# Delta heads of a hybrid decoder trunk: two places in ScalarE's order, the places of four weight sums, and the engine that makes the first mixer's

## The reference, cut to what matters

```
u = _rmsnorm(h, norm_mix[layer]).astype(jnp.float32) * valid
(a_q, a_f, a_i, a_g, b_qkv, b_beta, b_decay, b_g,
 c_q, c_k, c_v, c_gk, c_g, gate_logits) = jnp.split(u @ w_in[layer], split_points, axis=-1)
...
def _gated_deltanet(qkv_in, beta_in, decay_in, g_in, conv_w, a_log, dt_bias, norm_w, valid):
    qkv = jax.nn.silu(_causal_conv(qkv_in, conv_w))
    q, k, v = jnp.split(qkv, [B_HEADS * B_DK, 2 * B_HEADS * B_DK], axis=-1)
    q = _l2norm(_split_heads(q, B_HEADS)) * (B_DK ** -0.5)
    k = _l2norm(_split_heads(k * valid, B_HEADS))
    ...
    o = _chunk_gated_delta(q, k, v, log_a, beta)
    return _gated_head_norm(o, g_in, norm_w)
...
gates = jax.nn.sigmoid(gate_logits.reshape(b, total, N_BRANCH, d))
proj = jnp.einsum('blne,ned->blnd', ys, w_branch[layer])
merged = jnp.sum(gates * proj, axis=2)
```

## Time and profile before

| what | value |
|---|---|
| median of 3 runs | 1083.44 us (1082.18 to 1084.93) |
| the profiled execution, its own time | 1080.85 us |
| its span | 1079.0 us |
| PE busy | 1029.5 us, 95% |
| DVE busy | 536.2 us, 50% |
| ACT busy | 309.4 us, 29% |
| POOL busy | 68.4 us, 6% |

### The profile page before, as it was taken

The page is one execution under the profiler, slowest core; times in us unless marked ns, Lnnn a source line. Parts: engine busy times, 40 slices in busy tenths (PEclk is TensorE's granted clock), DMA queues, the critical chain, the costliest instruction groups (busy, mean ns, idle before and its releaser), DMA issues. The chain is left out here.

```text
span 1079.0 us, 20473 instructions
## 1 busy us (share of the span) xinstructions
PE 1029.5 (95%) x8841; PEld 695.6 (64%) x8841; DVE 536.2 (50%) x1074; ACT 309.4 (29%) x573; POOL 68.4 (6%) x73
## 2 busy tenths in 40 slices
PE   9999999999999999999999999999998999887886
PEld 8676776786777877867846546544456665545544
DVE  5757565749469468478464455432344321111124
ACT  3545445334244333343333033010110111101013
POOL 3000000000000000000000000000001222211110
PEclk9999999999999999999999999999999999989899
DMA  9222222141331232132112212163937999999976
GB/s 265 68 66 60 59 61 79 41 100 43 80 70 53 60 83 61 40 84 61 51 49 74 64 42 78 39 272 123 388 122 286 415 413 414 415 416 416 416 305 244
DMA packets 111965, 174.73 MB, mean 162 GB/s; under 512 B 9011, under 2 KB 87100, under 8 KB 103554
## 3 DMA queue, kind: packets, MB, share of 16 engines
q1 hardware_dynamic: 99010, 134.93, 36.3%
q10 hardware_dynamic: 7136, 27.33, 6.4%
q0 software_dynamic: 5728, 11.14, 3.9%
HBM read 169.16 MB, written 12.60 MB: 168 GB/s over the span
## 5 line engine op out<-in xcount | busy, mean ns | idle before, releaser
L767 PE MATMUL ps<-arena 128*128 128x256 f32 x672 | 165.0, 388 | 0.0
L767 PEld LDWEIGHTS ps<-arena 128*128 128x128 f32 x672 | 121.2, 190 | 16.4
L800 PE MATMUL ps<-arena 128*128 128x512 f32 x288 | 128.2, 594 | 1.2 <-DVE arena L1814 1.2
L797 PE MATMUL ps<-arena 128*128 128x264 f32 x400 | 123.1, 389 | 0.8 <-DVE gates L1558 0.8
L2299 PE MATMUL ps<-arena,gates 128*64 128x256 f32 (+1 forms) x1088 | 106.9, 355 | 15.8 <-DMA arena<-in_expert_w_up 15.3
L798 PE MATMUL ps<-arena 128*128 128x264 f32 x400 | 121.7, 386 | 0.0
L1441 DVE TENSOR_TENSOR arena<-arena 128x256 f32<-128x256 f32 (+6 forms) x198 | 94.3, 520 | 40.9 <-ACT arena L1237 27.6
L2299 PEld LDWEIGHTS ps<-arena,gates 128*64 128x64 f32 x1088 | 74.1, 145 | 54.5 <-DMA arena<-in_expert_w_up 23.1
L800 PEld LDWEIGHTS ps<-arena 128*128 128x128 f32 x288 | 53.6, 190 | 62.3 <-issue 61.8
L791 PE MATMUL ps<-yT,arena 128*128 128x512 f32 x192 | 84.8, 596 | 2.1 <-DVE gates L1558 1.4
L798 PEld LDWEIGHTS ps<-arena 128*128 128x128 f32 x400 | 76.0, 190 | 13.0
(11 more groups left out here) (370 smaller groups left out, 1341.2 us busy)
## 6 DMA issues: line engine op xcount, KB each, us to landing
arena<-in_w_in SPq DMA_DIRECT2D x68, 512.0 KB, 3.9
arena<-in_expert_w_gate SPq DMA_DIRECT2D x27, 1024.0 KB
arena<-in_expert_w_up SPq DMA_DIRECT2D x27, 1024.0 KB
arena<-in_expert_w_down ACTq DMA_DIRECT2D x16, 1024.0 KB, 33.1
arena<-in_w_branch SPq DMA_DIRECT2D x12, 512.0 KB, 4.0
arena<-in_expert_w_down SPq DMA_DIRECT2D x6, 1024.0 KB, 27.6
C<-in_expert_w_gate SPq DMA_DIRECT2D x5, 1024.0 KB
gates<-in_expert_w_up SPq DMA_DIRECT2D x5, 1024.0 KB
```

Of the source, the lines that this page charges most:

```text
L767: mm = t.matmul(dst, wt[:, k, :], rhs[:, k, :], start=(k == 0), stop=(k == KH - 1))
L797: t.matmul(dst[:, 0:HALF], wt, uT[:, k, 0:HALF], start=(k == 0), stop=(k == KD - 1))
L800: mm = t.matmul(dst, wt, uT[:, k, META:], start=(k == 0), stop=(k == KD - 1))
```

## The change

ACT's order in a delta head: `lnk` and `rik` now stand directly behind `kk`, ahead of `eg` and `E`. In heads 1 to 3 `gate_end` of the last pair ("c") of the head before stands ahead of `b_root`, not behind it. On PE the sum of squares of the head before (`ss`) comes after three pieces of the keys' next block and not four.

DVE's order in a delta head: `S1` of the pair "b" now stands ahead of `tk` and `S2` ahead of `km`; `S4` stands behind `tq`, ahead of `S3`. Before, `S1`, `S2` and `S4` stood together between `min` and `kn`.

In the heads of "a" the four sums leave DVE; POOL makes them, for heads 0 to 2 behind `mix_tokens` and for head 3 behind the DMA of the rows. The semaphore of the sums is split in two for that.

The diff, cut to its core:

```diff
@@ b_act, the list of ACT's steps
-  each(r, ["abk", "ek", "lk", "sk", "kk", "eg", "E", "lnk", "rik", "abq", ...
+  each(r, ["abk", "ek", "lk", "sk", "kk", "lnk", "rik", "eg", "E", "abq", ...
@@ mixers_gpsimd
+            def mix_weights(r):
+                n, p = pair_block("a", r), pair_no("a", r)
...
+                for m in (n, n + 1):
+                    g.wait_ge(sem(f"block_loaded{m % RING}"), (m // RING + 1) * 16)
+                if p:
+                    g.wait_ge(*pair_pe.after(f"P3.{p - 1}"))
+                g.tensor_tensor(s1, second[:, 0:KH], second[:, KH:], ALU.add).then_inc(*pair_mix.did(f"S1.{p}"))
...
             mix_tokens()
+            for r in range(A_R - 1):
+                mix_weights(r)
             g.wait_ge(*dve0.after("gbrow"))
             g.dma_start(rows_dram, token_rows).then_inc(sem("rows_sent"), 16)
             g.wait_ge(sem("rows_sent"), 16)
+            mix_weights(A_R - 1)
@@ mixers_tensor
             for r in range(B_R):
-                fill(4)
+                fill(3)
                 if r:
                     b_sum(r - 1)
@@ mixers_scalar
                     b_square(r - 1)
+                    gate_end("c", r - 1)
                     b_root(r - 1)
-                    gate_end("c", r - 1)
@@ mixers_vector, heads of "a"
-                        mix_weights("S1", "a", r)
-                        mix_weights("S2", "a", r)
-                    if l == 2:
-                        mix_weights("S4", "a", r)
-                        mix_weights("S3", "a", r)
@@ mixers_vector, delta heads
+                mix_weights("S1", "b", r)
                 less("k", b_em[:, 0:TOK], ck, b_em[:, 0:TOK], r)
+                mix_weights("S2", "b", r)
                 unit("k", b_kf, ck, b_em, r)
...
-                mix_weights("S1", "b", r)
-                mix_weights("S2", "b", r)
-                mix_weights("S4", "b", r)
                 v.wait_ge(*b_act.after(f"rik.{r}"))
...
                 less("q", b_nw[:, 0:TOK], cq, b_nw[:, 0:TOK], r)
+                mix_weights("S4", "b", r)
                 mix_weights("S3", "b", r)
```

More of the change, by code:

```diff
@@ L500, in hybrid_trunk @@
                                 each(r - 1, ["oo", "ln", "ri"] if r else []) +
-                                each(r, ["abk", "ek", "lk", "sk", "kk", "eg", "E", "lnk", "rik", "abq", "eq", "lq", "sq", "qq",
+                                each(r, ["abk", "ek", "lk", "sk", "kk", "lnk", "rik", "eg", "E", "abq", "eq", "lq", "sq", "qq",
                                          "N", "abv", "ev", "lv", "sv", "abg", "eg2", "lg", "Z1", "sg"] +
@@ L540, in hybrid_trunk, with mixed @@
                       each(C_R - 1, c_finish_names()))
-        pair_mix = Order("pair_weights", [f"{n}.{p}" for p in range(PAIRS) for n in ("S1", "S2", "S4", "S3")])
+        pair_mix = Order("pair_weights", [f"{n}.{p}" for p in range(A_R) for n in ("S1", "S2", "S4", "S3")])
+        delta_mix = Order("delta_weights", [f"{n}.{p}" for p in range(A_R, PAIRS) for n in ("S1", "S2", "S4", "S3")])
+        def mixed(name, p):
+            return (pair_mix if p < A_R else delta_mix).after(f"{name}.{p}")
         pair_pe = Order("pair_products", [f"{n}.{p}" for p in range(PAIRS) for n in ("P1", "P5", "P6", "P3")])
@@ L658, in mix_tokens @@
                 g.tensor_tensor(t4, u[1][0], t2, ALU.subtract).then_inc(*tokens_mixed.did("T4"))
+            def mix_weights(r):
+                n, p = pair_block("a", r), pair_no("a", r)
+                first, second = ring[:, n % RING, :, :], ring[:, (n + 1) % RING, :, :]
+                s1, s2, s4 = (mixed_w[:, m] for m in range(3))
+                for m in (n, n + 1):
[3 more added lines that the diff above has]
+                g.tensor_tensor(s1, second[:, 0:KH], second[:, KH:], ALU.add).then_inc(*pair_mix.did(f"S1.{p}"))
+                g.wait_ge(*pair_mix.after(f"S1.{p}"))
+                g.tensor_tensor(s2, s1, first[:, 0:KH], ALU.subtract).then_inc(*pair_mix.did(f"S2.{p}"))
+                g.wait_ge(*pair_mix.after(f"S2.{p}"))
+                g.tensor_tensor(s4, first[:, KH:], s2, ALU.subtract).then_inc(*pair_mix.did(f"S4.{p}"))
+                g.tensor_tensor(second[:, 0:KH], first[:, 0:KH], second[:, 0:KH], ALU.subtract).then_inc(*pair_mix.did(f"S3.{p}"))
             mix_tokens()
+            for r in range(A_R - 1):
+                mix_weights(r)
             g.wait_ge(*dve0.after("gbrow"))
@@ L739, in pair_step @@
                             t.wait_ge(*tokens_mixed.after("T4"))
-                        t.wait_ge(*pair_mix.after(f"S1.{p}"))
+                        t.wait_ge(*mixed("S1", p))
                         if stage == "c":
@@ L745, in pair_step @@
                     if name == "P6":
-                        t.wait_ge(*pair_mix.after(f"S2.{p}"))
+                        t.wait_ge(*mixed("S2", p))
                         t.wait_ge(*pair_copy.after(f"P1.{p}"))
                     if name == "P3":
-                        t.wait_ge(*pair_mix.after(f"S4.{p}"))
+                        t.wait_ge(*mixed("S4", p))
                         if stage == "c":
@@ L754, in pair_step @@
                     if name == "P7":
-                        t.wait_ge(*pair_mix.after(f"S3.{p}"))
+                        t.wait_ge(*mixed("S3", p))
                         t.wait_ge(*pair_sum.after(f"U2.{p}"))
@@ L1334, in mixers_scalar @@
                 a.activation(b_kb, b_kf, ACT.Square).then_inc(*b_act.did(f"kk.{r}"))
+                a.wait_ge(*b_pe.after(f"ssk.{r}"))
+                a.activation(b_em, pair(4), ACT.Ln, bias=eps_c).then_inc(*b_act.did(f"lnk.{r}"))
+                a.wait_ge(*b_act.after(f"lnk.{r}"))
+                a.activation(b_em, b_em, ACT.Exp, scale=-0.5).then_inc(*b_act.did(f"rik.{r}"))
                 a.wait_ge(*b_dve.after(f"dif.{r}"))
@@ L1338, in mixers_scalar @@
                 a.activation(b_es, b_es, ACT.Exp).then_inc(*b_act.did(f"E.{r}"))
[L1339 to L1342, removed]
                 a.wait_ge(*b_dve.after(f"q3.{r}"))
@@ L1509, in mix_weights @@
                 if name in ("S2", "S4"):
-                    v.wait_ge(*pair_mix.after({"S2": "S1", "S4": "S2"}[name] + f".{p}"))
+                    v.wait_ge(*delta_mix.after({"S2": "S1", "S4": "S2"}[name] + f".{p}"))
                 if p and name != "S3":
@@ L1513, in mix_weights @@
                 if name == "S3":
-                    v.wait_ge(*pair_mix.after(f"S4.{p}"))
+                    v.wait_ge(*delta_mix.after(f"S4.{p}"))
                 out_, a_, b2, op = {"S1": (s1, second[:, 0:KH], second[:, KH:], ALU.add), "S2": (s2, s1, first[:, 0:KH], ALU.subtract),
@@ L1517, in mix_weights @@
                                     "S3": (second[:, 0:KH], first[:, 0:KH], second[:, 0:KH], ALU.subtract)}[name]
-                v.tensor_tensor(out_, a_, b2, op).then_inc(*pair_mix.did(f"{name}.{p}"))
+                v.tensor_tensor(out_, a_, b2, op).then_inc(*delta_mix.did(f"{name}.{p}"))
             def gate_second(stage, r):
```

## The result

| what | before | changed |
|---|---|---|
| median | 1082.81 us (4 runs, 1080.88 to 1084.93) | 1071.65 us (4 runs, 1070.46 to 1071.85) |
| ratio of the runs | 1 | 0.9894, 95% interval 0.9874 to 0.9915 |
| profiled execution, span | 1079.0 us | 1070.0 us |

The changed kernel is faster by 11.2 us between the medians, 11.5 by the ratio (0.0106 x 1082.8). So the way and the mechanism came out as forecast, and the size came out at or past the fast end of the range. Most of what follows is about the 2 us between the forecast gain and the measured one.

The account below looks back on a forecast made before the run. PE was taken as the bound, losing time in delta heads to waits at KK, Z1 and ssk. Head 0 2.3 plus heads 1 to 3 7.05 made 9.4 us: median 1083.44 to 1074.1, range 1071.5 to 1079.5; forecast chance 62%.

Parts of the forecast that it names:

- The step that failed: End of the sum: profiled execution, going from 1080.85 to 1071.5 us, stands 2.6 under the median, giving 1074.1.
- The range's fast end: 1071.5 us: 2.6 us more if hidden 0.16 us losses also exist in the first mixer's levels and earlier DVE frees some.
- The terms of the sum: PE waits in delta heads: KK 1.19, Z1 0.77, ssk 0.39 us in heads 1 to 3; head 0 1.54 + 0.77.
- `rik` and the sums together hold `kb`: Delta heads, ahead of KK: ACT's late `rik` and DVE's three sums (2.14 us) fill the same time; either edit alone fails.
- `kn` at 321.0, 3.2 earlier; 1.7 us of cover at KK: Delta head 1: `kb` ends at 322.75, PE reaches KK at 324.43; KK's wait goes, 1.19 us per head in 1 to 3.
- The keys' chain 1.6 earlier: Start of delta heads 1 to 3: `km` and `kk` come 1.6 us earlier, `S1` sticking out 0.2; ssk's 0.39 wait goes.
- Z1's wait goes with 0.25 to spare: Delta heads behind KK: `U` 2.45 us earlier, `Db` ends at 338.3, PE reaches Z1 at 338.55; the 0.77 wait goes.
- The first mixer at zero: First mixer: 16 sums moved from DVE to POOL, estimated 1.2 us each there, gain and cost PE nothing.
- One: Delta heads: Z1's wait stays because PE or ACT held something between `U` and `Db`; gain 6.3 us, 1077.1; chance 15%.
- two: Delta heads: `S1` and `S2` lie on the key chain, ssk late, Z1's wait stays; gain about 4 us, 1079.4; chance 8%.
- Three: Expert phase: the gain is given back waiting for weights whose stream has a fixed end; 1083.4, no change; chance 9%.
- Four: First mixer: POOL's sums hold DVE where its steps alternate with ACT's; 9.4 us slower, 1092.8; chance 6%.

Follow-up runs that it names:

- the added step: Changed kernel plus one unread 128x512 product on DVE between `U` and `Db` of each delta head: 1073.08 us against 1082.16 for before, ratio 0.9921.
- the sums placed at their worst: Changed kernel with POOL's first-mixer sums held back until DVE has made the gate product, to run beside the levels: 1071.31 us against 1081.64 for before, ratio 0.9899.
- The three series: Changed kernel against before, first measurement and two repeats without edits: 1071.65 us against 1082.81; 1070.43 against 1082.87; 1072.56 against 1081.94.
- the second profile of before: The kernel before, timed and profiled again with no edit: 1082.99 us against 1082.87, ratio 1.0004; profiled span 1078.9 us.

## Why the prediction was right, and where it was not

The mechanism was right in every wait that it named. What failed is a size, and in the main one step of the sum:

- **The step that failed** is the last one: "it stands 2.6 under the median of the runs shown, so the median goes from 1083.44 to 1074.1". It handed the distance of one execution on to the changed kernel. For the profiled execution the sum gave 1071.5, and 1071.85 was measured; but this execution stands 0.2 over its median of 1071.65 and not 2.6 under it. The other two profiled executions of the changed kernel stood 2.0 under and 0.3 over theirs. Of the 2.4 us between 1074.1 and 1071.65, 0.6 come from the median of three runs, which was 1082.81 with the fourth and 1082.87 with 29 later ones; 0.4 are terms of the sum that were too small (below); the other 1.4 us, the surplus of this series, stay open.
- **The range's fast end** allowed for one cause alone, hidden losses in the first mixer. They do not exist: 206.16 us from the small columns to ssk of head 0, before and after. It left nothing for the scatter of stalls, setup and expert phase that the runs shown before, 1082.18 to 1084.93, already hinted at.
- **The terms of the sum were sized too small.** Each wait was priced as its idle time plus about 0.16 us of overlap. At KK and ssk the first group behind the wait is also passed through 0.1 us more slowly. By starts KK gave 1.19 + 0.11, ssk 0.40 + 0.10, and Z1 0.70 and not 0.77. Heads 1 to 3: 2.48 against 2.35; head 0 2.33 against 2.31; the sum 9.8 against 9.4.
- **`rik` and the sums together hold `kb`: right.** In ACT's and DVE's orders apart, one edit gave 0.27 us per head and the other cost 0.55, as the step "either edit alone would leave the other in the way" has it.
- **`kn` at 321.0, 3.2 earlier; 1.7 us of cover at KK: right.** Measured from ssk's start the change is the same: `kn` begins 318.39 - 315.51 = 2.88 us behind it, worked out 2.97. Cover 1.65.
- **The keys' chain 1.6 earlier: right** in its effect, ssk's wait is gone. Against V1's start `kk` is 1.8 earlier: `S1` fits into DVE's pause and does not stick out by 0.2. Without this part a head loses 0.67 us, not 0.39, as the cover at Z1 goes with it.
- **Z1's wait goes with 0.25 to spare: right,** 0.26 by the trace and 0.3 by the added step.
- **The first mixer at zero: right in the number, with a thin reason.** A POOL sum, taken as half of 2.36, was 1.27 measured, and up to 2.34 where DVE held POOL. The sums did hold DVE, but behind a cover of PE that I had not worked out; I had only DVE's pauses.
- **Rivals.** One and two did not come: the waits at Z1 and at ssk are gone. Three: the third mixer to the end takes 532.2 to 534.3 us in the changed kernel and 532.9 to 533.7 before, so nothing was given back. Four: shown in mechanism; 0.54 us in all reached PE with the sums placed at their worst, nothing as the change has them.

**What stays open.** The three series give 11.5, 12.1 and 9.6 us (ratios 0.9894, 0.9888, 0.9911), the clean landmarks 9.8. The first and third interval hold 9.8 (a ratio of 0.9909); the second ends at 0.9906. By the mean of the three, weighted with their runs, about 1 us more is gained than the landmarks account for. Whether that is chance or something that timed executions have and the profiled ones lack, these runs do not settle: no segment of any profile shows it, without POOL's part the ratio is the same, and the stalls are in both kernels. Too few executions are profiled to say whether they are rarer or shorter in one of them.

## What to carry to other kernels

Where two engines' queues each hold the same step, price the edits only as a pair: each alone here was worth -1 or +2 us, both about -8. Read a wait's price from start to start of the groups around it, and look whether the group behind the wait runs slower too. And take the distance of one profiled execution to the median as scatter, to be put into the range at both ends, not as a constant that the changed kernel inherits.

## What the runs showed of the hardware

Contention of DVE and POOL goes both ways. POOL, then DVE, of the changed kernel at the start of head 1 of the first mixer:

```profile
72.10 1.27 POOL L672 TENSOR_TENSOR arena<-arena 128x512 f32<-128x512 f32 x1 [36.83 <-DMA arena<-in_w_in]
73.45 2.13 POOL L674 TENSOR_TENSOR arena<-arena 128x512 f32<-128x512 f32 x1
75.65 1.27 POOL L676 TENSOR_TENSOR arena<-arena 128x512 f32<-128x512 f32 x1
```

```profile
72.64 1.80 DVE L1572 SCALAR_TENSOR_TENSOR gates<-gates,yT 128x1024 f32<-128x1024 f32 x1 [3.40 <-ACT yT L1205]
74.37 1.24 DVE L1682 TENSOR_TENSOR bcol<-bcol,valid 128x20 f32<-128x20 f32 x1
```

The first DVE step takes 1.23 us alone, as in the kernel before, and 1.80 here; POOL's first sum runs for the first 0.73 of it. POOL's second sum takes 2.13 and not 1.27, with DVE's step still running in its first microsecond, and the 20-column step, 0.17 us alone, ends with that sum at 75.6. The Trainium skill ("SBUF — State Buffer", section "Who interferes with whom") describes such an exclusive hold between a DVE instruction with two SBUF inputs and a GpSimd instruction that reads SBUF; these rows agree, for a SCALAR_TENSOR_TENSOR too.

The other surprise is the stalls of PE in the levels of delta head 2. In twelve of the fourteen profiles head 2 is longer than head 1, by 0.27 to 2.02 us. Where a stall is long enough for a row, it stands ahead of the last 12 or the last 22 matmuls of two groups, 0.4 to 1.25 us each, at the same places of the program in the changed kernel and its variants, with DVE's sums alone (1.25 us ahead of the last 12) and with POOL's sums alone, which has one of 0.50 us in head 0 too. The 0.3 us of the second profile of before and of ACT's order alone are lost in the same levels. The profile names nothing that PE waited for. What they are was not tested.
